# Gated recurrence of block two: ScalarE opens each unit, and the carry and the take stand one level later

## The reference

```
f   = lb + (1 - lb) * sigmoid(f_pre)          # decay of every channel, per token
k   = (1 - lb) * sigmoid(-f_pre)
S_t = diag(f_t) S_{t-1} + k_t v_t^T
o_t = S_t^T q_t
```

## Time and profile before

| | us |
|---|---|
| median of 3 executions | 3597.81 (3596.05 to 3600.88) |
| profiled execution | 3596.66 |
| its span in the profile | 3594.8 |
| PE busy in it | 3327.1 (93%) |
| DVE busy | 1702.4 (47%) |
| ACT busy | 1181.5 (33%) |
| POOL busy | 962.3 (27%) |
| mean granted PE clock | 0.955 of full speed |

### The profile page before, as it was taken

How to read it: one execution, slowest core, us unless ns; L and a number is a source line. 1 busy time by engine, 2 the same in 40 slices (tenths; PEclk the granted TensorE clock), 3 DMA queues, 4 the chain that set the end, 5 groups by cost and what they waited for, 6 DMA issues and landing times. The chain is left out here.

```text
span 3594.8 us, 42433 instructions
## 1 busy us (share of the span) xinstructions
PE 3327.1 (93%) x17158; PEld 2642.7 (74%) x17158; DVE 1702.4 (47%) x2635; ACT 1181.5 (33%) x1920; POOL 962.3 (27%) x412
## 2 busy tenths in 40 slices
PE   5999989988999799999999777989999888899998
PEld 4887667866888688888888664368887664578887
DVE  6995467554332323355510897552211585653211
ACT  3223364324443422122231224333222323543222
POOL 0001322432444122322332110024444221024443
PEclk7999999998999899999999998989999888899999
DMA  4222324451223222333321000012233110023332
GB/s 188 99 97 86 130 99 154 154 176 59 95 98 93 74 88 84 128 135 131 134 73 57 30 18 7 1 65 94 95 111 96 48 52 27 1 65 94 100 94 88
DMA packets 91790, 315.99 MB, mean 88 GB/s; under 512 B 10822, under 2 KB 12614, under 8 KB 90314
## 3 DMA queue, kind: packets, MB, share of 16 engines
q1 hardware_dynamic: 88876, 304.74, 25.8%
q10 hardware_dynamic: 2720, 8.55, 0.6%
HBM read 311.16 MB, written 2.10 MB: 87 GB/s over the span
## 5 line engine op out<-in xcount | busy, mean ns | idle before, releaser
L261 POOL TENSOR_TENSOR terms<-streams,terms 128x1024 fp32r<-128x1024 f32 (+2 forms) x408 | 962.1, 2358 | 2613.1 <-ACT terms L249 2613.1
L519 PE MATMUL bank<-terms,terms 128*128 128x512 f32 (+2 forms) x3776 | 1407.5, 373 | 24.2 <-POOL terms L261 10.3
L520 PE MATMUL bank<-terms,terms 128*128 128x512 f32 (+2 forms) x3776 | 1401.9, 371 | 0.0
L521 PE MATMUL bank<-terms,terms 128*128 128x512 f32 (+2 forms) x3776 | 1400.4, 371 | 0.0
L249 ACT ACTIVATE terms<-streams 128x1024 fp32r<-128x1024 f32 (+1 forms) x462 | 475.5, 1029 | 1741.6 <-PE bank L521 1494.0
L519 PEld LDWEIGHTS bank<-terms,terms 128*128 128x128 f32 x3776 | 715.5, 189 | 159.5 <-issue 30.9
L521 PEld LDWEIGHTS bank<-terms,terms 128*128 128x128 f32 x3776 | 715.0, 189 | 121.9
L520 PEld LDWEIGHTS bank<-terms,terms 128*128 128x128 f32 x3776 | 716.1, 190 | 119.1
L1946 DVE TENSOR_TENSOR stage<-stage,bank 128x256 f32<-128x256 f32 (+1 forms) x84 | 51.8, 618 | 544.4 <-ACT stage L1924 544.4
L1319 DVE SCALAR_TENSOR_TENSOR arena<-arena,vec 128x512 f32<-128x512 f32 x240 | 162.5, 745 | 0.2
L1910 DVE TENSOR_TENSOR terms<-stage,terms 128x512 fp32r<-128x512 f32 (+1 forms) x66 | 114.3, 1735 | 0.0
(11 more groups left out here) (379 smaller groups left out, 3476.8 us busy)
## 6 DMA issues: line engine op xcount, KB each, us to landing
streams<-in_ffn_w SPq DMA_DIRECT2D x104, 512.0 KB, 3.5
streams<-in_w_mod SPq DMA_DIRECT2D x72, 512.0 KB, 3.6
streams<-in_w_up SPq DMA_DIRECT2D x44, 512.0 KB, 3.5
streams<-in_w_gu SPq DMA_DIRECT2D x44, 512.0 KB, 3.5
streams<-in_w_ada SPq DMA_DIRECT2D x32, 512.0 KB, 3.5
streams<-in_w_down SPq DMA_DIRECT2D x32, 512.0 KB, 3.5
streams<-in_w_v SPq DMA_DIRECT2D x24, 512.0 KB, 3.7
streams<-in_ffn_w SPq DMA_DIRECT2D x24, 384.0 KB, 3.3
```

What stands on the lines that cost most here:

```text
L261: gp.tensor_tensor(self.low(m), self.raw(n), self.high(m), ALU.subtract).then_inc(self.low_made.sem, 1)
L519: pe.matmul(out, high[:, at], x_high, start=kk == start, stop=False)
L520: pe.matmul(out, high[:, at], x_low, start=False, stop=False)
L521: mm = pe.matmul(out, low[:, at], x_high, start=False, stop=kk == kts - 1)
```

## The change

Each unit's opening leaves DVE. ACT's gates apply the two affine steps themselves, with Identity activations on pre and key. A new helper begin on ACT does three things for the unit that comes next: it copies the key half of the key's latent part into both[1] (level 1's key product, since suf would be 1 there), copies the query half of pre into suf's key half (which is suf's first lengthening), and fills suf's query half with 1. begin(n + 1) stands on ACT behind place and ahead of keep, and waits for the gates, for the scores of level 7 and for the end of the unit (ready). PE waits for its first step ahead of level 1, DVE for all three ahead of pre's first lengthening. carry moves behind level 2, PE's sums behind level 3, take behind level 4, and the gates of unit n + 1 wait for carry (states) instead of take.

```diff
             def gates(n):
                 h, d = units[n]
-                act.activation(pres[n % 2], fpre[:, 2 * h + d, :], ACT.Sigmoid)
-                act.activation(keys[n % 2], fpre[:, 2 * h + d, :], ACT.Sigmoid, scale=-1.0).then_inc(gated.sem, 1)
+                pre, key, one = pres[n % 2], keys[n % 2], k.v("lb1", 4 * d + h)
+                act.activation(pre, fpre[:, 2 * h + d, :], ACT.Sigmoid).then_inc(opened.sem, 1)
+                act.activation(key, fpre[:, 2 * h + d, :], ACT.Sigmoid, scale=-1.0).then_inc(opened.sem, 1)
+                act.wait_ge(*opened(2 * n + 1))
+                act.activation(pre, pre, ACT.Identity, bias=k.v("lb0", 4 * d + h), scale=one)
+                act.wait_ge(*opened(2 * n + 2))
+                act.activation(key, key, ACT.Identity, scale=one).then_inc(gated.sem, 1)
+
+            def begin(n):
+
+                if n >= len(units):
+                    return
+                h, d = units[n]
+                qh, kh = 1 - d, d
+                def halves(ap):
+                    return ap.rearrange("p (b s) -> p b s", s=2)
+                x, p4, s4, k4 = halves(both[1]), halves(pres[n % 2]), halves(suf), halves(keys[n % 2])
+                act.wait_ge(*gated(n + 1))
+                if n:
+                    act.wait_ge(*scored(8 * n))
+                    act.wait_ge(*ready(9 * n))
+                act.activation(x[:, :, kh], k4[:, CTX // 2:, kh], ACT.Copy).then_inc(begun.sem, 1)
+                act.activation(s4[:, :, kh], p4[:, :, qh], ACT.Copy).then_inc(begun.sem, 1)
+                act.activation(s4[:, :, qh], p4[:, :, qh], ACT.Identity, bias=1.0, scale=0.0).then_inc(begun.sem, 1)
...
             gates(0)
+            begin(0)
             for n in range(len(units)):
                 inputs.keep_context(act, n, tiled)
                 if n + 1 < len(units):
                     if n:
-                        act.wait_ge(*taken(n))
+                        act.wait_ge(*states(n))
                     gates(n + 1)
                 place(n, levels - 1)
                 place(n, levels)
+                begin(n + 1)
                 inputs.keep(act, n)
...
                     pe.wait_ge(*ready(9 * n + lev + 1))
+                    if lev == 1:
+                        pe.wait_ge(*begun(3 * n + 1))
...
                     inputs.multiply(pe, n, lev, tiled)
-                    if n and lev == 1:
+                    if n and lev == 3:
                         sums(n - 1)
...
-                one = k.v("lb1", 4 * d + h)
                 dve.wait_ge(*gated(n + 1))
-                dve.tensor_scalar(pre, pre, one, k.v("lb0", 4 * d + h), ALU.mult, ALU.add)
-                dve.memset(suf, 1.0)
-                link(dve.tensor_scalar(key, key, one, None, ALU.mult))
                 dve.sem_inc(ready.sem, 1)
...
+                    if lev == 1:
+                        dve.tensor_tensor(x[:, :, qh, :], q4[:, :, qh, :], p4[:, nctx:, qh, :], ALU.mult
+                                          ).then_inc(ready.sem, 1)
+                        dve.wait_ge(*ready(9 * n + 2))
+                        dve.wait_ge(*begun(3 * n + 3))
+                        link(dve.tensor_tensor(p4[:, :, qh, :], p4[:, :, qh, :], p4[:, :, kh, :], ALU.mult))
+                        if n >= 2:
+                            dve.wait_ge(*placed(2 * n - 2))
+                        merge(n, 0)
+                        continue
...
-                    if lev == 1:
-                        if n:
-                            carry(n - 1)
-                        if n >= 2:
-                            dve.wait_ge(*placed(2 * n - 2))
-                        merge(n, 0)
-                    if n and lev == 3:
+                    if n and lev == 2:
+                        carry(n - 1)
+                    if n and lev == 4:
                         take(n - 1)
```

More of the change, by code:

```diff
@@ L153, in __init__ @@
         self.squared_early = sig("squared_early")
+        self.begun = sig("begun")
         self.ahead_high = sig("ahead_high")
@@ L2141, in stage_hgrn @@
     B = k.bank
-    tiled = k.more[11]
+    tiled, opened, begun = k.more[11], k.more[15], k.begun
     units = [(h, d) for h in range(HEADS2) for d in range(2)]
@@ L2345, in stage_hgrn @@
     for s, m in ((gated, n), (ready, 9 * n), (scored, 8 * n), (merged, 6 * n), (placed, 2 * n), (turned, n), (turn_copied, n),
-                 (kv_done, n), (states, n), (summed, n), (taken, n), (tiled, 2), (k.dve_done, len(links))):
+                 (kv_done, n), (states, n), (summed, n), (taken, n), (tiled, 2), (k.dve_done, len(links)),
+                 (opened, 2 * n), (begun, 3 * n)):
         s.counted(m)
```

## The result

The kernel after the change takes 3613.11 us (median of 4 runs, 3612.94 to 3617.78) against 3596.93 us before (4 runs, 3591.76 to 3600.88): ratio 1.0048 [1.0035, 1.0060], slower by 16 us. Forecast was 3605.7, slower by 7.9. The profiled execution took 3612.94 us with a span of 3611.1 (before 3594.8).

A forecast was written before the change was run, and what follows sets the result against it. DVE bounds the stage before the change, PE's chain to level 0's merge after it. Sum: 3597.81 + 1.4 (chain, net) + 6.5 (clock) = 3605.7 us, 0.22% slower; forecast's own range 3602 to 3608, wider range 3593.5 to 3614.

The forecast's parts named there:

- What is taken from DVE: Gated recurrence, per unit: opening 2.04 us, level-1 key product 2.26, suf product 0.66; together 4.96 of 24.72 us.
- The chain: Unit's end to level 0's merge: begin delays ACT's copies and PE, merge at +6.28, unit 24.96 us, seven turns +1.7.
- rival D: ACT's strided activations cost up to double, 8.5 us in all: 3607.7 us without clock falls; chance 0.06.
- rival E: DVE stays the bound, PE not held up: unit 23.23 us and kernel 3587, or down to 3563; chance 0.09.
- The start of the stage: Ahead of level 1, DVE's 2.04 us become two ACT activations of about 0.9: a gain of 0.2 to 0.4 us.
- The clock: PE's longer pause behind the transposes brings the lower clock in four turns of seven, 1.63 us each: +6.5 us.
- take asks for the sums a whole DVE level later: no wait: With sums behind level 3 and take behind level 4, DVE's take would not wait for PE: no cost.
- The tail: Last unit's stretch behind its last key product: unchanged, since begin returns at once.
- Rival C: Clock falls at every turn, 11.4 us, kernel 3610.6, with 1 us or more on top in some turns; chance 0.20.
- A: The forecast: PE's chain takes DVE's place, clock falls at two to five turns, 3602.5 to 3607.3 us; chance 0.42.

The follow-up runs named there:

- the delayed kernel: Kernel before plus three needless ACT copies ahead of keep, where the change has begin; nothing else of the change: 3607.28 us, ratio 1.0025.
- filled pauses: Changed kernel plus needless matmuls in PE's pauses: 3 ahead of the unit's end, 11 behind the transposes, 7 behind level 2: 3601.25 us, ratio 1.0009.
- Begin behind the copies: Changed kernel with ACT's begin(n + 1) moved behind the two key copies instead of ahead of keep: 3601.77 us, ratio 1.0002.
- the run again: Changed kernel unaltered, measured once more on another chip beside the kernel before: 3616.46 us, ratio 1.0052.
- the two experiments with units of 24.71 and 26.48: Changed kernel with begin behind the key copies (3601.77 us); changed kernel with 11 needless matmuls behind the transposes only (3607.39 us).
- the run with 3, 3 and 7 fillers: Changed kernel with begin behind the key copies, carry behind level 2, needless matmuls ahead of unit's end, behind transposes, behind level 2: 3589.63 us, ratio 0.9976.
- the gates alone: Kernel before with only a unit's decay and key finished by ACT instead of DVE, begin's work left on DVE: 3593.64 us, ratio 0.9981.

## Why the prediction was right in its direction and wrong in its size

- **What is taken from DVE**: right. Busy per unit 18.9 us (forecast 18.6), no key product at 2.34 us. POOL's subtraction takes 2.35 us in all units instead of 3.40: DVE is idle beside it. The Trainium skill, SBUF — State Buffer, section "SBUF: two separate sides", has DVE, with two inputs in SBUF, and POOL contend for a port pair that whichever starts first keeps for its whole instruction. The traces agree: here, as the prediction said, the subtraction "finds DVE waiting", and the delayed kernel has the stall back, with a product that started 0.03 us behind POOL's. So these two engines meet at more than semaphores, as the key product of 2.34 us in the earlier trace rows already shows.
- **The chain**: right. In the first turn, at full clock, the copies end at +3.68, kv starts at +3.73, level 0 ends at +6.24 and the merge starts at +6.35 (forecast +3.63, +3.68, +6.18, +6.28). A unit of 24.93 us there (less the take's wait), and 24.99 to 25.41 in all seven with filled pauses (forecast 24.96). The strided activations cost next to nothing, as taken: 0.45, 0.54 and 0.53 us (forecast 0.40, 0.51 and 0.60), so rival D falls. The two gate activations with pointers take 1.02 and 0.92 us (forecast about 0.92 each), off the path. Begin behind the copies gives 23.20, by rival E's own arithmetic. Rival E as such falls: the chain was held up.
- **The start of the stage**: -0.8 us in this execution and -0.2 in the run again (21.84 and 22.49 against 22.65), forecast -0.3: right within that scatter.
- **The clock**: the step that failed, in count and price. The prediction put it at 4 x 1.63 = 6.5 us. It was six falls at the turn, each of 2.14 us on the chain, and one of 1.52 ahead of the take: 14.4 us. With some 0.8 us of smaller effects in the slowed units the seven are 15.2 us above those with filled pauses (190.86 - 175.69). The price was wrong because I took it from the turn in the earlier trace rows, where the clock fell within the 12 kv matmuls (2.85 us) and rose within level 0 (1.49). Behind the long pause both groups ran at 0.50 from end to end (2.93 and 1.92). The count I had left between one and seven, and chose the middle without a reason. What spoke to it is the longer pause: 2.73 us and more instead of the 0.96 of the earlier trace rows. The prediction also had the same two pauses in every turn. In the first two turns of the kernel before they are 0.24 and 1.28 us, since PE has more of the projection to do there. In the changed kernel the first pause is 0.23 us at most in those two turns, and with 2.74 and 2.88 us behind the transposes the clock fell in three of the four turns of its two profiled executions. So the pause ahead of the transposes is not needed for a fall.
- **"take asks for the sums a whole DVE level later: no wait"**: wrong wherever the clock fell ahead of level 3. I costed carry behind level 2 as DVE's 2.04 us and did not ask what PE does meanwhile. It pauses ahead of level 3 for 1.73 to 1.94 us in the changed kernel and for 1.93 to 2.02 in the experiments at full clock. Before, PE waited for carry too, ahead of the sums, but 0.98 to 1.30 us, and the clock held there in all those units. A fall behind the longer pause costs 1.5 us (the two experiments with units of 24.71 and 26.48).
- **The tail**: forecast unchanged, measured +2.8 us, also of the clock, so that the lower clock cost 17.9 us in units and tail against the 6.5 forecast. Its pauses are as before (0.93, 0.96 and 2.07), yet kv took 2.64 us there and each group of sums 0.63 instead of 0.39:

```profile
2194.90 0.88 PE L2273 MATMUL bank<-ident,arena 128*128 128x128 f32 x6 [0.93 <-DVEq L2370]
2196.74 2.64 PE L2278 MATMUL bank<-arena,stage 128*128 128x128 f32 x12 [0.96 <-ACT stage L2234]
2201.45 0.77 PE L2245 MATMUL bank<-sq,arena 128*128 128x128 f32 x2 [2.07 <-DVEq L2308]
```

The run again had it too (11.16 us). With all pauses filled the tail is 8.37 us, but there the first of its own pauses holds three filler matmuls as well. With only the pause behind the transposes filled, which puts nothing into the tail, it is 8.36 us at full clock. And in the run with 3, 3 and 7 fillers, three of them in the tail's first pause, its sums fell all the same (8.96 us). So filling in the tail is neither needed nor enough, and the cause stays open.

Rival C came nearest (a fall at every turn, 3610.6, "1 us or more on top"). The Trainium skill, TensorE: Matmul & The Clock Gate, section "HAM oscillation — how this bites in real kernels", tells of a kernel in which waits of 3 to 5 us between short bursts brought the low clock back before each burst. Here a shorter pause did so almost as often: behind 2.73 to 3.15 us the clock fell in 13 turns of 14 in two profiled executions. Behind 0.96 to 1.30 us it fell in 3 turns of 28 (the kernel before, the gates alone, and begin behind the copies with carry in either place). I gave C 0.20 and should have given it most of A's share.

Left open: what decides a single turn (the pair of rows from the delayed kernel), why the pause ahead of level 3 brought five falls in one experiment and two in another, why the tail's clock falls behind unchanged pauses, and where the kernel loses its clock in the slower cluster of whole runs, with the change and without it.

## What to carry to other kernels

When an edit lengthens the wait of PE between two short groups of matmuls, price the groups behind it at the lower clock from end to end, in every turn, until a trace shows otherwise; and look for every pause that a moved instruction makes on PE, not only for what it costs on its own engine. Work that another engine is to take over early belongs behind whatever that engine already owes the chain: with the pauses filled, the same three activations made a unit 25.0 us ahead of the key copies and 23.2 behind them. Where a pause must stay, needless matmuls in it (here 21 a unit) tell what the clock costs, and took the ratio from 1.0048 to 1.0009, 14 of the 16 us.

## What the runs showed of the hardware that was not expected

- With 43 more records of matmuls in a unit (x166 against x123 in unit 3) the stage was 17.3 us shorter, and the instructions of the other engines took no longer beside them (in unit 3 DVE 18.87 us, ACT 7.75, POOL 2.35, against 18.95, 7.74 and 2.35).
- Six transposes (0.88 us of PE) between two pauses did not keep the clock up, where 11 filler matmuls behind them, which left 0.3 to 0.7 us of the second pause, did in all seven turns.
- The same pauses of 0.92 and 2.59 us led to a fall in one turn and to none in another of the same execution.
